# The mixing of the first block, rebuilt: state space by chunks of four tokens, attention by pairs of heads

## What is computed

```python
h = h + 0.5 * swiglu(rmsnorm(h, norm_ffn1), ffn1_w1, ffn1_w3, ffn1_w2)
z = rmsnorm(h, norm_mix) @ w_in        # q (8 heads of 64), kc vc ks vs kw vw (2 kv heads), gates, u
o_nsa = nsa_attention(...)             # three branches, weighed by the gates:
                                       #  compressed (15 blocks), selected and window
o_s5 = s5_mixer(u, ...)                # 32 groups of 16 inputs and 64 complex states
h = h + concatenate([o_nsa, o_s5]) @ w_out
h = h + 0.5 * swiglu(rmsnorm(h, norm_ffn2), ...)
h = h + sigmoid(rmsnorm(h, norm_ple) @ w_ple_gate) * (p @ w_ple)
```

## Time and profile before

| | |
|---|---|
| runs | 1794.58, 1791.44, 1793.86 us; median 1793.86 |
| profiled execution, its own time | 1786.83 us |
| its span | 1785.1 us, mean granted TensorE clock 0.952 |
| busy | PE 1611.5, PEld 1377.5, DVE 981.5, ACT 732.6, POOL 318.2 us |
| chain that ended last | PE 76%, DVE 10%, ACT 6%, DMA 3%, issue 3%, POOL 2% |
| DMA | 223.16 MB, mean 125 GB/s |

### The profile page before, as it was taken

How to read it: one execution, slowest core, us unless ns; L and a number is a source line. 1 busy time by engine, 2 the same in 40 slices (tenths; PEclk the granted TensorE clock), 3 DMA queues, 4 the chain that set the end, 5 groups by cost and what they waited for, 6 DMA issues and landing times.

```text
span 1785.1 us, 25335 instructions
## 1 busy us (share of the span) xinstructions
PE 1611.5 (90%) x9504; PEld 1377.5 (77%) x9504; DVE 981.5 (55%) x1537; ACT 732.6 (41%) x1266; POOL 318.2 (18%) x286
## 2 busy tenths in 40 slices
PE   5999979798999998899889898999998999988996
PEld 4899977444899997686668777788874887868996
DVE  4888872785488875534543145333333636435554
ACT  4333373233544435524542336222233446445443
POOL 3999554233300004001100000000000001010000
PEclk9999999798999999999989899999999999989998
DMA  7677755000677774132112112233321232224662
GB/s 250 197 238 227 235 173 179 25 1 13 217 237 244 243 237 129 47 89 78 36 36 71 59 48 83 86 103 106 106 94 48 94 107 83 91 63 136 203 201 87
DMA packets 79187, 223.16 MB, mean 125 GB/s; under 512 B 6656, under 2 KB 32256, under 8 KB 78464
## 3 DMA queue, kind: packets, MB, share of 16 engines
q1 hardware_dynamic: 54528, 195.20, 34.0%
q10 hardware_dynamic: 24576, 26.82, 4.8%
HBM read 220.94 MB, written 1.05 MB: 124 GB/s over the span
## 4 chain that ended last, share of the span: by engine, by line
PE 76%; DVE 10%; ACT 6%; DMA 3%; issue 3%; POOL 2%; SPq 1%; DVEq 0%; ACTq 0%
PE ps L445 62%; DMA ring<-stream 3%; PE ps L455 2%; DVE w_lo L386 1%; ACT w_hi L968 1%; ACT area L1158 1%; PE ps L789 1%; POOL w_lo L386 1%; PE ps L830 1%; PE ps L583 1%; PE ps L773 1%; PE ps L847 1%; DVE area L1502 1%; DVE area L1497 1%; PE ps L810 1%
## 5 line engine op out<-in xcount | busy, mean ns | idle before, releaser
L445 PE MATMUL ps<-hn_hi,w_hi 128*128 128x256 f32 (+1 forms) x1952 | 635.2, 325 | 62.6 <-DVE w_lo L386 31.0
L445 PE MATMUL ps<-hn_lo,w_hi 128*128 128x256 f32 (+1 forms) x1952 | 624.5, 320 | 0.0
L445 PE MATMUL ps<-hn_hi,w_lo 128*128 128x256 f32 (+1 forms) x1952 | 623.7, 319 | 0.0
L386 DVE TENSOR_TENSOR w_lo<-ring,w_hi 128x1024 fp32r<-128x1024 f32 (+1 forms) x316 | 387.6, 1230 | 376.9 <-ACT w_hi L968 373.6
L968 ACT ACTIVATE w_hi<-ring 128x1024 fp32r<-128x1024 f32 (+1 forms) x347 | 359.7, 1037 | 389.9 <-DMA ring<-stream 279.7
L445 PEld LDWEIGHTS ps<-hn_hi,w_hi 128*128 128x128 f32 x1952 | 380.0, 195 | 95.6 <-DVE w_lo L386 33.9
L445 PEld LDWEIGHTS ps<-hn_lo,w_hi 128*128 128x128 f32 x1952 | 380.2, 195 | 24.0
L445 PEld LDWEIGHTS ps<-hn_hi,w_lo 128*128 128x128 f32 x1952 | 379.4, 194 | 24.6
L1015 ACT ACTIVATE area<-ps 128x512 f32<-128x512 f32 (+1 forms) x168 | 82.1, 499 | 330.8 <-PE ps L445 325.5
L386 POOL TENSOR_TENSOR w_lo<-ring,w_hi 128x1024 fp32r<-128x1024 f32 x31 | 80.0, 2599 | 287.1 <-ACT w_hi L968 287.1
L1849 POOL TENSOR_SCALAR_AFFINE_SELECT area<-area 128x512 f32<-128x512 f32 x8 | 5.0, 621 | 611.7 <-ACT area L1212 611.7
(11 more groups left out here) (273 smaller groups left out, 2029.3 us busy)
## 6 DMA issues: line engine op xcount, KB each, us to landing
ring<-stream SPq DMA_DIRECT2D x359, 512.0 KB, 3.7
mod_at<-mod_stream ACTq DMA_DIRECT2D x46, 512.0 KB, 5.3
pk<-pack ACTq DMA_DIRECT2D x1, 1610.0 KB, 7.1
pk<-pack SPq DMA_DIRECT2D x1, 1549.0 KB, 12.2
h<-x_in SPq DMA_DIRECT2D x1, 1024.0 KB, 4.9
cond_at<-cond SPq DMA_DIRECT2D x2, 512.0 KB, 14.2
mod_at<-mod_stream SPq DMA_DIRECT2D x2, 512.0 KB, 12.5
hc<-ctx_in ACTq DMA_DIRECT2D x1, 1024.0 KB, 9.1
```

The costliest lines, as they stand in the source:

```text
L386: eng.tensor_tensor(lo[:, 0:w], raw, hi[:, 0:w].bitcast(F32), ALU.subtract).then_inc(lo_ready[who], 1)
L445: m = pe.matmul(dst, w_, x_, start=(start and n == 0), stop=(stop and n == 2), skip_group_check=True)
```

## The change

- The state space goes by chunks of `CH` = 4 tokens: GpSimd builds powers `bpow`, `cpow` (36 products and sums of 512 columns beyond the first powers) and tables for 64 chunks only; TensorE turns four `bpow` (`turn_input`), makes matrices `lag` for the terms inside a chunk (`lags`), and for each of four groups j of four state tiles runs `s5_in(j)` (32 matmuls of 64 or 63 columns and 32 rows) and `s5_out(j)` (32 matmuls of 32 output rows and 64 columns, and 6 with `lag`). VectorE works on four tiles at once (`states_in`, `states_scan`, `states_back`, `state_space`), products back by the tables included, which GpSimd made before.
- These pieces stand between the projection units on TensorE. The `cmpk` and `cmpv` units alternate.
- Attention takes the two kv heads of one query tile and one branch together (8 pairs). The probabilities are normed in place by VectorE. `glu`, the compressed scores and the first pair's scores stand ahead of the steps, and `wout` 0 and 1 are multiplied together, from tile 4 on, while attention ends.
- ScalarE's sine of the angles comes after the fifth step of the first net, no longer after the first.
- In layer 1 of the second block, the high and low parts of `ymrg` are made inside the merge loop, in other memory (`merged_parts`).
- The expression that fills `LOW`, and the calls of `low_until`, are rewritten.

The diff, cut:

```diff
-    _who = "dve" if _name[0] in ("ffn1", "ffn2") or len(_name) > 1 and UNIT[_name] >= UNIT["dk", 0, 0] else "pool"
+    _who = "pool" if "u" in _name[:1] or UNIT["kc",] <= UNIT[_name] < UNIT["ffn2", "w1", 0] or _name[0] == "pleg" else "dve"
...
+        def merged_parts(l, k):
+            if l == 0:
+                return hn_hi[:, k, :], hn_lo[:, k, :]
+            return early_hi[:, k, :], free_halves[k // 4][:, k % 4, T:2 * T]
...
+            def s5_in(j):
...
+                for part in range(2):
+                    for q in range(CH):
+                        for r in range(4):
+                            rows = slice(32 * r, 32 * r + 32)
+                            o = bank(4 + r, NC * part, NC)
+                            w = bT[rows, q, part, P * j:P * j + P]
+                            if q == 0:
+                                m = pe.matmul(o, w, uT[rows, j, 0, :], start=True, stop=False, skip_group_check=True)
+                            else:
+                                m = pe.matmul(o[:, 1:NC], w, uT[rows, j, CH - q, 0:NC - 1], start=False, stop=(q == CH - 1),
+                                              skip_group_check=True)
...
+            def s5_out(j):
...
+                for t in range(CH):
+                    for part in range(2):
+                        for r in range(4):
+                            pe.matmul(ps[32 * r:32 * r + 32, 512 * b + NC * t:512 * b + NC * t + NC],
+                                      cpow[:, 4 * j + r, part, 32 * t:32 * t + 32], x[:, part, r, :],
+                                      start=(t == 0 and part == 0), stop=(t == 0 and part == 1), skip_group_check=True)
...
+            turn_input(0)
+            turn_input(1)
+            project(("u", 2))
+            project(("u", 3))
+            turn_input(2)
+            turn_input(3)
+            project(("kc",))
+            project(("vc",))
+            lags()
+            s5_in(0)
+            project(("q", 0))
...
+            project(("ks",))
+            s5_out(0)
+            s5_in(1)
+            project(("kw",))
+            rotate(2)
+            project_gates(0)
+            rotate(3)
+            project_gates(1)
+            s5_out(1)
+            s5_in(2)
+            project_gates(2)
+            s5_out(2)
+            s5_in(3)
...
+            for step in range(2, 11):
+                if step < 8:
+                    scores(step)
+                if step <= 9:
+                    turn(step - 2)
+                if step >= 3:
+                    weigh(step - 3)
...
+            low_until(("vc",))
+            pool.wait_ge(s("lags_made"), 1)
+            pool.memset(blk, 0.0).then_inc(s("blk_cleared"), 1)
             pool.memset(kbd, 0.0).then_inc(s("blk_cleared"), 1)
-            low_until(("vg", 2))
...
+            low_until(("wout", KT - 1))
```

More of the change, by code:

```diff
@@ L36 @@
 BW = 512
+CH = 4
+NC = T // CH
 EPS = 1e-6
@@ L685, in _ @@
-            for i in range(NST + 2):
-                if i < NST:
-                    s5_in(i)
-                    scores(i)
-                if 1 <= i <= NST:
-                    turn(i - 1)
-                if 1 <= i <= NST:
-                    s5_out(i - 1)
-                if i >= 2:
-                    weigh(i - 2)
             for cc_ in range(2):
@@ new lines, in _, with fill @@
+            act.wait_ge(s("lag_cleared"), 1)
+            for r in range(4):
+                rows = slice(32 * r, 32 * r + 32)
+                m = act.activation(lag[rows, :, :, 32 * r:32 * r + 32],
+                                   bank(BANK["lags",][0], 0, 384)[rows, :].rearrange("p (j l o) -> p l j o", j=4, l=CH - 1), ACT.Copy)
+            m.then_inc(act_evac, 1)
+            take(("q", 0), zq[:, 0, :])
+            load_mod(act, 26)
+            take(("q", 1), zq[:, 1, :])
+            def fill(kv, src):
```

810 lines of the change are left out of this document (487 added, 323 removed).

## The result

| | before | changed |
|---|---|---|
| median of four runs | 1794.22 us | 1735.33 us (1730.80 to 1736.11) |
| ratio | | 0.9669 (95% interval 0.9648 to 0.9689) |
| profiled execution, own time | 1786.83 us | 1736.11 us |
| its span | 1785.1 us | 1734.4 us |

The prediction was 1741 in a range of 1712 to 1768, and the time was 1735: 58.9 us less than before by the medians, 50.7 by the two spans. The sum of its terms was 53. The 7.0 us added for the median above the profiled execution did not come again (1735.33 for 1736.11). And the terms were not right one by one. A plan of the span shows it; "net 1 over" is the start of VectorE's last updates of `h` in the first net, "net 2 begins" TensorE's first matmul of the second net.

The account below looks back on a forecast made before the run. TensorE was taken to bound the nets, and hand-overs round four engines the mixing. Gains of 11 (first net), 40 (to `wout` 2) and 2 (merge), 53 off 1786.8, gave 1734; the median 7.0 above made 1741, range 1712 to 1768.

Parts of the forecast that it names:

- Term 1: First net: moving the sine behind the fifth step ends TensorE's 9.1 us wait, 6.4 of other waits stays; gain 11.
- Term 2: Projections with the state space inside: TensorE's work 94 us, plus 4.5, 4 and 8, ends `s5_out(3)` at 350.
- Term 3: From the end of `s5_out(3)` to the exponentials: the small chain with `glu` in it takes 14 us, to 364.
- Term 4: Attention: eight pairs at 3.9 us, 31, plus 7, 5 and 5; `wout` 2 starts at 412, 40 us earlier.
- Term 5: Layer 1's merge: TensorE's idle time there shrinks, gain 2 us (0 to 4).
- 1: State space and compressed units: each change of row or column group drains the array, 320 changes, slower, 1837; chance 0.05.
- 3: State space and head pairs: no quarters side by side, `s5_in` 7.7 us for 3.3, pairs 4.9, 1762; chance 0.12.
- 4: First net: its stall only moves, to late loads, +9 us, 1750; chance 0.1.
- 5: Mixing, better: quarters at half price (-7), clock kept (-5), contention light (-6), small chain overlapped (-5), 1718; chance 0.18.
- 2: Projections: VectorE and GpSimd block each other, the full 21.4 us, a second group waits some 5 more, 1759; chance 0.2.

## Why the prediction was right in sum and wrong in parts

**Term 1, the first net (forecast +11, measured -12): wrong.** The first half, "the wait of 9.1 goes", was right and rather low: alone it gave 13.6. The step that failed is the next one, "8.0 x 125 / 157.5 = 6.4 stays". It took TensorE's loss as in proportion to GpSimd's busy time, whatever GpSimd does. The runs put in its place: 36 products of two operands and 512 columns cost 17 to 21 us; of one operand 1.4; halved 7.1. GpSimd was busy 129.9 us, near the 125 forecast, and TensorE waited 21.9 us for the 6.4. The old tables were two thirds instructions of one operand and all of 256 columns, the new ones are the dearest kind. The row that could have warned me was there: the earlier trace rows shows a short product of two operands at 2.52 us, and I used it for the projections alone.

**The rule of the Trainium skill** (SBUF — State Buffer, "Who interferes with whom"), that a VectorE instruction with two SBUF operands and a GpSimd instruction reading SBUF exclude each other for the whole instruction, I had weighed in the wrong place. In the first net the traces agree with it for GpSimd's two-operand products (2.11 us for 1.22, in turns), and only in part for the one-operand ones (1.42, and VectorE unhindered for two instructions running).

**Term 2, the projections (forecast end at 350 of the old span, 111 us from the first projection; measured 96.3, and 102.4 in the run with the heads one after the other).** The prices of the state space were too high: a group in at 3.3 took 1.94, one out at 4.6 took 2.5, `lags` at 4 took 1.5:

```profile
276.36 1.50 PE ps L575 x64
...
277.91 0.95 POOL area L2089
...
278.92 3.18 POOL w_lo L408
...
300.81 1.03 PE ps L611 x64
301.84 1.48 PE ps L616 x12
303.32 0.38 PE ps L594 x8
303.70 0.67 PE ps L596 x24
304.37 0.22 PE ps L594 x8
304.59 0.67 PE ps L596 x24
```

In, 64 instructions take 0.38 + 0.67 + 0.22 + 0.67 = 1.94, or 0.03 each, not 0.05. "The row of the smallest matmuls is nearest" was the wrong choice: that row ran alone, and these run four abreast. That is worth 5 us in, 2.5 for `lags` and 8 out. The 4 us for changes of shape were not seen: the chain has no gap at them, and the first eight instructions of a group in took only 0.16 us more than the same eight in its middle. Of the 8 us for blocking by GpSimd one instruction shows on the chain, `area` at line 1593 with 2.70 us, 2.3 too long: 5.7 less. Against this stand three things that I had at nothing or too low: the wait for GpSimd's clearing and low part, 2.4 (the rows from 277.91 on; I had written "nothing is left to pay", since `s5_in`(0) was to cover it, but it lasted 1.94 us for 3.3, and the low part 3.18 for 2.4 to 2.6); the compressed units at 13.5 for 11, with a load 2.8 us late; and stretches at the lower clock (the first pair of units took 7.3 for 5.8 at a granted clock of 0.80 from 254 to 261.5; the third out 4.7 for 2.5 and the last group in 3.6 for 1.94, at 0.50 from 325.9 to 334.2), 5 us. The wait for the states was sized rightly, 4.9 for 4.5, but stood elsewhere: 0.8 before `s5_out`(1), 4.1 before `s5_out`(2), none before `s5_out`(3). Part of the 96.3 is chance: the run with the heads one after the other has the same instructions here, waited 7.4 us for the states and took 6 us longer.

**Term 3 (forecast 14): right.** The first exponential came 13.0 us behind `s5_out`(3), at 363.4.

**Term 4 (forecast 48 from there to `wout` 2, measured 39.4).** `wout` 2 began at 402.8, forecast for "near 400 in the new span". The steps were 3.66 us apart, not 3.9; from maxima to maxima of two pairs 7.32:

```profile
380.56 0.42 DVE area L1689
...
387.88 0.42 DVE area L1689
```

Eight of them and the tail took 33.8, where I had 31 + 7 + 5 with the low clock, and the 5 for table, high and low part of `wout` 2 passed beside the first pair of `wout` (5.6 us). The halves side by side, 3.5 against 4.9 a pair, hold by the rows of two kernels above: a pair's scores take what one head's took. That they need to be issued in turn for it does not hold.

**Term 5 (forecast 2): right.** TensorE waits 2.8 us there instead of 4.5, a gain of 1.7; the 3.1 of the table lie within what that long stretch varies by.

**The rivals.** 1 fell: 320 changes of quarter cost nothing that shows. The Trainium skill (TensorEngine Tiling (Array Packing), "Key Properties") says that different tiles work independently; the 1.94 against 5.41 us agrees. 3 fell too, for the quarters by the run, for the pairs by the rows. 4 fell: after the sine alone the loads kept up. Of the four savings that 5 named, the quarters and the light contention came. 2 had the right mechanism, VectorE and GpSimd blocking each other, in the wrong stage: it struck in the first net. Without that it would have been 5 that came, near 1721 by the ratio of the run with the products on VectorE; and once the net is short, the blocking does show in the projections, with four instructions of 2.5 to 2.9 us before `s5_out`(0):

```profile
266.30 2.63 DVE L1644 TENSOR_TENSOR area<-area 128x256 f32<-128x256 f32 x1
...
274.93 2.51 DVE L1658 TENSOR_TENSOR area<-area 128x256 f32<-128x256 f32 x1
```

(the run with the products on VectorE, in order of time; alone such a product takes 0.42.)

## What to carry to other kernels

Work on an engine that has nothing to do is not free when its instructions and those of a full one hold each other up: cost it by what it does to the neighbour, by form and operands of its instructions and by when it does it, not by its own busy time. Here 36 products cost 17 to 21 us on the idle engine and 2 on the busy one. And check a prediction by its terms even when the sum comes out: here the first net and the mixing were each off by about 20 us, and the plan of the span showed it where the total did not.

## What was not expected of the hardware

- A GpSimd product of two SBUF operands over 512 columns (1.05 us at its shortest) and VectorE's low parts go in turns: 2.02 and 2.11 us. A GpSimd instruction of one operand over 512 columns takes 1.5 to 1.8 us beside VectorE, and VectorE's mean rises to 1.42 only. GpSimd's busy time for the 36 hardly differs, 65 and 61 us.
- Two-operand products cut to 256 columns stretched the same low part to 1.66 us. VectorE was busy nearly as long as with the whole ones, 177.2 for 180.4 us, and TensorE lost a third as much.
- An instruction of a float32 matmul of 64 columns took 0.030 us where neighbours used different row quarters, 0.085 where they used the same; with column quarters 0.016 and 0.049. For two halves with two products each, the order made no difference.
- The stretch from the second net to the end varied from 1299.9 to 1307.6 us between kernels with the same instructions there, the first net's end by 4 us, and the waits for the states by 2.5. A gain of 2 us can't be read from one span, and from a wait only against a second run of the same instructions.
